# A transformer kernel's gate and up projections as 2x2 block products: seven of 256 columns in place of four of 512

## The chip, the core and the metric

The kernel runs on one core of one Trainium2 chip. Its time is the device time of one execution in microseconds (us). The engines are TensorE (PE in the rows; its weight loads are PEld), VectorE (DVE), ScalarE (ACT), GpSimd (POOL) and SyncE (SP), which issues most of the DMAs. Each engine works through its own list in order; they meet by semaphores.

## What is computed

Two layers of a transformer block and a third block of another kind, on one sequence of 512 tokens and 1024 features. The change is in the feed-forward part of the first two layers:

```python
D_FF = -(-(8 * D_MODEL) // (3 * 256)) * 256        # 2816 = 22 x 128
h2 = rmsnorm(x, norm_ffn[l])
gu = jnp.einsum('btd,df->btf', h2, w_gate_up[l])
g, up = jnp.split(gu, 2, axis=-1)
x = x + jnp.einsum('btf,fd->btd', jax.nn.silu(g) * up, w_down[l])
```

## The kernel before

All of it is kept transposed: features on the 128 partitions, the 512 tokens along a row. Single precision is reached with three matmuls for each block of weights: weights and activations are each split into a rounded part and the rest (`wh`, `wl` and `hh`, `hl`), and `three` and `tile` (L1769 to L1771) add high by high, high by rest and rest by high into one bank of PSUM.

Weights arrive as chunks of 128 x 1024 numbers (512 KB) in a stream that SP loads into two buffers `raw` (L370); ACT rounds a chunk into one of four slots of `wh` (L572), POOL subtracts to get `wl` (L418), and TensorE uses it. The chunks of a layer are those of its mixing part, eight of the output projection (WO), 44 of gate and up and 22 of down. A gate/up chunk holds the 1024 inputs of 128 output features: 8 blocks, so 24 matmuls of 512 columns. A gate chunk and its up chunk are a *pair*; a layer has FT = 22.

The gate/up stage is a loop of 11 trips with two pairs each on TensorE, DVE and ACT. For a pair DVE multiplies both banks with `rstd`, the token's inverse norm (L1384, L1386), ACT takes silu of the gate (L805), DVE multiplies the two (L1389), ACT rounds the product into `ah` (L808), DVE subtracts for `al` (L1391). The four banks go round, so TensorE writes a bank again two pairs later and waits for L1384 or L1386 to have read it. The down stage follows: 22 chunks, each of 24 matmuls with `ah` and `al`, which are kept for all 22 pairs. During it DVE also works at the modulation of the third block: 24 products with the tensor `ada`, loaded by ACT (L1398).

## Time and profile before

| | |
|---|---|
| three timed runs | 2154.14, 2154.64, 2156.37 us (median 2154.64) |
| the profiled execution, first to last instruction | 2152.9 us |
| the same less the median | -1.7 us (its time outside the span is not listed apart) |
| TensorE busy | 2143.8 us (100%), granted clock 1.000 |
| DVE / ACT / POOL busy | 1198.8 (56%) / 939.4 (44%) / 1064.0 us (49%) |
| gate/up stage of layer one and of layer two | from 302.7 to 542.7 and from 958.6 to 1198.9 us |
| DMA | mean 102 GB/s |

A duration of a matmul in the rows is that of one through the whole array; the next one starts before it ends, so the rate is read from the distance of two starts. "Busy" counts such overlap once. The granted clock is 1.00 where TensorE has its full 2.4 GHz.

### The profile page before, as it was taken

What the parts mean: (1) busy time and instruction counts of PE and PEld (TensorE: products, weight loads), DVE (VectorE), ACT (ScalarE), POOL (GpSimd) and SP (SyncE); (2) the same over time, 40 slices, a digit from 0 to 9 for tenths busy, and PEclk for the clock granted to TensorE, in tenths of its full rate; (3) what the DMA queues carried; (4) which work ended last, traced back from release to release, by engine and by line L of the source; (5) the groups of instructions that cost most, each with busy time, mean ns of one, the idle gap of its engine ahead of it and who ended that gap; (6) DMA issues with size and microseconds to landing.
All of it is one profiled execution on the core that took longest, in us unless ns stands there. A gap on an engine that the chain in (4) does not pass through costs nothing.

```text
span 2152.9 us, 29052 instructions
## 1 busy us (share of the span) xinstructions
PE 2143.8 (100%) x10406; PEld 1727.3 (80%) x10406; DVE 1198.8 (56%) x1581; ACT 939.4 (44%) x1517; POOL 1064.0 (49%) x559
## 2 busy tenths in 40 slices
PE   9999999999999999999999999999999999999999
PEld 7877788888888877788888888877787678888887
DVE  7988863222446987864222445759887746333201
ACT  5656543222214556634333215426645655444311
POOL 4973335444444983344444453433766754444442
PEclk9999999999999999999999999999999999999999
DMA  5432223333753332233333672322221012333332
GB/s 184 112 92 68 78 79 112 94 96 97 235 194 97 104 97 69 69 98 98 93 94 95 208 224 85 98 70 68 77 90 50 30 59 89 104 94 94 98 98 88
DMA packets 62869, 219.57 MB, mean 102 GB/s; under 512 B 7936, under 2 KB 8192, under 8 KB 62784
## 3 DMA queue, kind: packets, MB, share of 16 engines
q1 hardware_dynamic: 55728, 193.25, 29.1%
q10 hardware_dynamic: 7056, 25.17, 3.6%
q8 instruction: 54, 0.88, 0.2%
q14 instruction: 31, 0.25, 0.0%
HBM read 212.76 MB, written 2.10 MB: 100 GB/s over the span
## 4 chain that ended last, share of the span: by engine, by line
PE 94%; DVE 3%; POOL 2%; ACT 1%; issue 1%; POOLq 0%; DVEq 0%; ACTq 0%
PE bank L1769 29%; PE bank L1771 28%; PE bank L1770 28%; PE bank L1953 1%; PE bank L1979 1%; PE bank L2014 1%; POOL soft_lo L516 1%; PE bank L1987 0%; DVE soft_hi L1659 0%; POOL wl L418 0%; PE bank L2267 0%; PE bank L2342 0%; PE bank L2398 0%; DVE bank L1620 0%; PE bank L1861 0%
## 5 line engine op out<-in xcount | busy, mean ns | idle before, releaser
L418 POOL TENSOR_TENSOR wl<-raw,wh 128x1024 fp32r<-128x1024 f32 x317 | 771.8, 2436 | 849.3 <-ACT wh L572 849.2
L1769 PE MATMUL bank<-hh,wh 128*128 128x512 f32 (+1 forms) x1979 | 772.1, 390 | 0.9 <-DVE hl L1469 0.6
L1771 PE MATMUL bank<-hh,wl 128*128 128x512 f32 (+1 forms) x1979 | 762.7, 385 | 0.0
L1770 PE MATMUL bank<-hl,wh 128*128 128x512 f32 (+1 forms) x1979 | 762.2, 385 | 0.0
L572 ACT ACTIVATE wh<-raw 128x1024 fp32r<-128x1024 f32 x349 | 368.0, 1055 | 574.3 <-PE bank L1771 509.8
L1769 PEld LDWEIGHTS bank<-hh,wh 128*128 128x128 f32 x1979 | 371.8, 188 | 81.3 <-issue 7.2
L1770 PEld LDWEIGHTS bank<-hl,wh 128*128 128x128 f32 x1979 | 372.0, 188 | 75.1 <-issue 2.2
L1771 PEld LDWEIGHTS bank<-hh,wl 128*128 128x128 f32 x1979 | 371.7, 188 | 75.1
L1769 PE MATMUL bank<-ah,wh 128*128 (+1 forms) x512 | 199.2, 389 | 0.0
L1770 PE MATMUL bank<-al,wh 128*128 (+1 forms) x512 | 199.2, 389 | 0.0
L1771 PE MATMUL bank<-ah,wl 128*128 (+1 forms) x512 | 199.2, 389 | 0.0
L425 POOL TENSOR_TENSOR wl<-raw,wh 128x512 fp32r<-128x512 f32 x64 | 85.2, 1353 | 133.1 <-ACT wh L572 133.1
L1160 DVE SCALAR_TENSOR_TENSOR bank<-glu,par,bank 128x512 f32<-128x512 f32 x180 | 135.9, 755 | 5.8
L1386 DVE TENSOR_TENSOR tmp<-bank,rstd 128x512 f32<-128x512 f32 x44 | 30.4, 691 | 188.2 <-PE bank L1771 188.2
L1769 PEld LDWEIGHTS bank<-ah,wh 128*128 128x128 f32 x512 | 96.1, 188 | 20.1
L1770 PEld LDWEIGHTS bank<-al,wh 128*128 128x128 f32 x512 | 96.1, 188 | 20.0
L1771 PEld LDWEIGHTS bank<-ah,wl 128*128 128x128 f32 x512 | 96.1, 188 | 19.8
L1398 DVE SCALAR_TENSOR_TENSOR ada_acc<-ada_w,cond,ada_acc 128x1024 f32<-128x1024 f32 x42 | 64.8, 1544 | 83.2 <-DMA ada_w<-ada 82.6
L808 ACT ACTIVATE ah<-tmp 128x512 f32 x44 | 27.8, 631 | 182.5 <-DVE tmp L1389 182.5
L710 ACT ACTIVATE prob<-bank,neg_max,q_scale 128x128 f32<-128x128 f32 x128 | 56.9, 454 | 74.2 <-DVE neg_max L1228 74.2
L440 POOL TENSOR_TENSOR conv<-conv,th 128x512 f32<-128x512 f32 x60 | 77.6, 1294 | 13.6 <-ACT th L644 9.3
L1384 DVE TENSOR_TENSOR tmp<-bank,rstd 128x512 f32<-128x512 f32 x44 | 30.4, 690 | 91.5 <-PE bank L1771 90.9
(391 smaller groups left out, 2734.6 us busy)
## 6 DMA issues: line engine op xcount, KB each, us to landing
raw<-stream SPq DMA_DIRECT2D x351, 512.0 KB, 3.6
ada_w<-ada ACTq DMA_DIRECT2D x48, 512.0 KB, 4.6
x<-x_t SPq DMA_DIRECT2D x4, 512.0 KB, 6.9
out_t<-x SPq DMA_DIRECT2D x8, 256.0 KB, 2.1
th<-q SPq DMA_DIRECT2D x16, 64.0 KB
th<-q SPq DMA_DIRECT2D x64, 16.0 KB
q<-th SPq DMA_DIRECT2D x16, 64.0 KB, 2.0
cst<-consts SPq DMA_DIRECT2D x1, 640.0 KB, 5.8
```

Of the source, the lines that this page charges most:

```text
L418: nc.gpsimd.tensor_tensor(wl[:, slot, :], raw[:, raw_slot, :], wh[:, slot, :].bitcast(F32), ALU.subtract).then_inc(lo_ready, 1)
L425: last = nc.gpsimd.tensor_tensor(wl[:, slot, at], raw[:, raw_slot, at], wh[:, slot, at].bitcast(F32), ALU.subtract)
L440: nc.gpsimd.tensor_tensor(conv[:, 1, :], conv[:, 1, :], th[:, 0, 4 + (j - 1) % 4, :], ALU.add).then_inc(tap_added, 1)
L572: af(wh[:, slot, :], raw[:, raw_slot, :], ACT.Copy).then_inc(hi_ready, 1)
L710: af(prob[:, g % 2, i, :], folded[:, i, :], ACT.Exp, bias=neg_max[:, g % 2, i:i + 1], scale=q_scale[:, at:at + 1], accum_out=den[:, g % 2, ...
L1160: link(stt(acc, glu[:, t, j:j + T], w, acc, ALU.mult, ALU.add))
L1384: tt(tmp[:, 2 + p, :], bank[:, b, :], rstd[:, :], ALU.mult).then_inc(lin_free, 1)
L1386: tt(tmp[:, 4 + p, :], bank[:, b + 1, :] if b < 3 else bank[:, 0, :], rstd[:, :], ALU.mult).then_inc(lin_free, 1)
L1398: stt(acc, w, c_k, acc, ALU.mult, ALU.add).then_inc(ada_used, 1)
L1769: mm(dst, wh[:, slot, w], xh, start=start, stop=False)
L1770: mm(dst, wh[:, slot, w], xl, start=False, stop=False)
L1771: return mm(dst, wl[:, slot, w], xh, start=False, stop=stop)
```

## The change

The gate/up stage of the two layers treats a pair as a 2x2 block product. The weights' blocks are: the first and the second half of the 1024 inputs, by gate and up. The activations' blocks are: the first and the second half of the inputs, by the left and the right 256 tokens. Where the plain product takes eight block products (here 48 matmuls of 512 columns, each of which does two of them at once), seven products of sums of blocks are enough. Each product is now 4 blocks x 3 matmuls of 256 columns.

- POOL forms four sums and differences of a pair's weight blocks, `mix` (`mix_up`, `mix_firsts`, `mix_three`, `mix_four`, each 128x512). Together with three blocks taken as they are they are the seven *items* of a pair.
- ACT rounds each item into a half slot of `wh` (`item_round`), DVE subtracts for the rest (`item_rest`; the first ten are done by POOL). Seven half slots go round, so an item is rounded once the same product of the pair before is done. The activations' sums (`set_h`, `set_l`) are made once in each layer, while WO runs.
- TensorE's order for pair p is: first(p), fifth(p), fourth(p-1), third(p-1), sixth(p), second(p), seventh(p). Two sets of three banks alternate between the pairs. Partial results that are used twice are copied out of PSUM by ACT (`snap`) and added by DVE (`gate_first_half`, `up_second_half`, `gate_second_half`), and `activate` multiplies up by silu(gate) in two halves. It reads the first bank of the pair; `first_product` of the pair two later writes this bank and waits for it.
- The products of gate and up are kept whole in `act_full`; scaling by `rstd`, rounding and the rest move into the down stage (`scale_act`, `act_hi`, `act_rest`), with four slots, between the 24 products with `ada`.
- The gate/up weights come from a tensor of their own, `ffn`, into four buffers. The loops of the stage are written out. Several semaphores are merged.

```diff
+        ITEM_HALF = [2, 4, 5, 6, 7, 0, 1]
+        S1, S3, S2, S4 = 0, 1, 2, 3
...
+                        sp.wait_ge(item_lo, n0 + at_second(p - 2))
+                        sp.wait_ge(mixed, s0 + N_SUMS * (p - 1))
+                    sp.dma_start(gate_raw(p), ffn[l * 2 * FT + 2 * p]).then_inc(tile_in[2 * (p % 2)], 16)
...
+                    elif p:
+                        sp.wait_ge(item_lo, n0 + at_fourth(p - 2))
+                    sp.dma_start(up_raw(p), ffn[l * 2 * FT + 2 * p + 1]).then_inc(tile_in[2 * (p % 2) + 1], 16)
...
+                def mix_up(p):
+                    pool.wait_ge(tile_in[2 * (p % 2) + 1], l * PAIR_LOADS + pair_landed(p))
+                    if p:
+                        pool.wait_ge(mixed, s0 + N_SUMS * p)
+                        pool.wait_ge(item_lo, n0 + at_fifth(p - 1))
+                    nc.gpsimd.tensor_tensor(mix[:, S1, :], up_raw(p)[:, 0:T], up_raw(p)[:, T:D], ALU.add).then_inc(mixed, 1)
...
+                def mix_four(p):
+                    pool.wait_ge(mixed, s0 + N_SUMS * p + 3)
+                    if p:
+                        pool.wait_ge(item_lo, n0 + at_third(p - 1))
+                    nc.gpsimd.tensor_tensor(mix[:, S4, :], gate_raw(p)[:, T:D], mix[:, S2, :], ALU.subtract).then_inc(mixed, 1)
...
+                for p in range(2, FT):
+                    mix_up(p)
+                    mix_firsts(p)
+                    mix_three(p)
+                    mix_four(p)
...
+                def item_round(n, src):
+                    if n > 7:
+                        act.wait_ge(product_done, n0 + n - 7)
+                    af(item_of(wh, n), src, ACT.Copy).then_inc(item_hi, 1)
...
+                def snap(p, i, dst):
+                    act.wait_ge(product_done, n0 + [at_first(p), at_sixth(p), at_seventh(p)][i])
+                    af(dst, bank[:, PAIR_BANKS[p % 2][0], LEFT], ACT.Copy).then_inc(snapped, 1)
...
+                for p in range(1, FT):
+                    more = p + 1 < FT
+                    snap(p, 0, sums_tmp(p)[:, LEFT])
+                    if more:
+                        round_first(p + 1)
+                        round_mixed(p + 1, S1, at_fifth(p + 1))
+                        round_fourth(p)
+                        round_mixed(p, S4, at_third(p))
...
+                    snap(p, 1, sums_tmp(p)[:, RIGHT])
+                    if more:
+                        round_mixed(p + 1, S2, at_sixth(p + 1))
+                    silu(p - 1)
+                    if more:
+                        round_second(p + 1)
...
+                    snap(p, 2, up_tmp(p)[:, LEFT])
+                    if more:
+                        round_mixed(p + 1, S3, at_seventh(p + 1))
...
-                with dve.Fori(0, FT // 2) as i:
-                    for p in range(2):
-                        b = (M_GU + 2 * p) % 4
-                        dve.wait_ge(used, i * 4 + (cg + 2 * p + 1))
...
+                def item_rest(n, src):
+                    dve.wait_ge(item_hi, n0 + n)
+                    tt(item_of(wl, n), src, item_of(wh, n).bitcast(F32), ALU.subtract).then_inc(item_lo, 1)
...
+                def up_second_half(p):
+                    dve.wait_ge(product_done, n0 + at_seventh(p))
+                    dve.wait_ge(snapped, 3 * (FT * l + p) + 3)
+                    dve.wait_ge(set_lo, set0 + N_SETS)
+                    tt(up_tmp(p)[:, RIGHT], up_tmp(p)[:, LEFT], bank[:, PAIR_BANKS[p % 2][2], LEFT], ALU.add).then_inc(pair_step, 1)
+
+                def gate_second_half(p):
+                    dve.wait_ge(product_done, n0 + at_third(p))
+                    tt(gate_tmp(p)[:, RIGHT], sums_tmp(p)[:, RIGHT], bank[:, PAIR_BANKS[p % 2][2], LEFT], ALU.add).then_inc(pair_step, 1)
+                    dve.wait_ge(pair_step, gate_second(l, p))
+                    tt(gate_tmp(p), gate_tmp(p), rstd[:, :], ALU.mult).then_inc(pair_step, 1)
+
+                def activate(p):
+                    dve.wait_ge(ffn_silu, FT * l + p + 1)
+                    tt(act_full[:, p, LEFT], bank[:, PAIR_BANKS[p % 2][0], LEFT], gate_tmp(p)[:, LEFT], ALU.mult)
+                    dve.wait_ge(pair_step, up_second(l, p))
+                    tt(act_full[:, p, RIGHT], up_tmp(p)[:, RIGHT], gate_tmp(p)[:, RIGHT], ALU.mult).then_inc(ffn_act, 1)
...
+                    item_rest(at_fourth(p), up_raw(p)[:, T:D])
+                    gate_second_half(p - 1)
+                    item_rest(at_third(p), mix[:, S4, :])
+                    if more:
+                        item_rest(at_sixth(p + 1), mix[:, S2, :])
...
+                    activate(p - 1)
+                    gate_first_half(p)
+                    if more:
+                        item_rest(at_second(p + 1), gate_raw(p + 1)[:, T:D])
+                    up_second_half(p)
+                    if more:
+                        item_rest(at_seventh(p + 1), mix[:, S3, :])
...
-                with pe.Fori(1, FT // 2) as i:
-                    for s in range(4):
-                        pe.wait_ge(lin_free, i * 4 + (mg + s - 3))
-                        tile(i * 4 + (cg + s), (cg + s) % RW, (M_GU + s) % 4, hh, hl)
...
+                def product(n, dst, xh, xl, start, before=lambda kk: None):
+                    pe.wait_ge(item_lo, n0 + n)
+                    high, low = item_of(wh, n), item_of(wl, n)
+                    for kk in range(4):
+                        before(kk)
+                        w = slice(kk * P, kk * P + P)
+                        mm(dst, high[:, w], xh[:, kk, :], start=start and kk == 0, stop=False, skip_group_check=not start)
+                        mm(dst, high[:, w], xl[:, kk, :], start=False, stop=False, skip_group_check=not start)
+                        last = mm(dst, low[:, w], xh[:, kk, :], start=False, stop=kk == 3, skip_group_check=not start)
+                    last.then_inc(product_done, 1)
...
+                def first_product(p):
+                    if p >= 2:
+                        pe.wait_ge(ffn_act, FT * l + p - 1)
+                    product(at_first(p), bank_of(p, 0), hh[:, 0:4, LEFT], hl[:, 0:4, LEFT], True,
...
+                def third_product(p):
+                    pe.wait_ge(pair_step, up_second(l, p))
+                    product(at_third(p), bank_of(p, 2), hh[:, 4:8, RIGHT], hl[:, 4:8, RIGHT], False)
+
+                for p in range(FT):
+                    first_product(p)
+                    fifth_product(p)
+                    if p:
+                        fourth_product(p - 1)
+                        third_product(p - 1)
+                    sixth_product(p)
+                    if p == 0:
+                        sum_of_squares(s0 + SQ_FFN + KT - 1)
+                    second_product(p)
+                    seventh_product(p)
```

The places at which it moves instructions:

DVE before, one pair in the loop of the gate/up stage (L1384 and L1386 read the banks of gate and up; L1391 is the rest of the activations):

```order
L1384 TENSOR_TENSOR tmp<-bank,rstd 128x512 [waits used]
L1385 REGISTER_ALU
L1386 TENSOR_TENSOR tmp<-bank,rstd 128x512 [waits used]
L1387 ISA
L1388 REGISTER_ALU [waits ffn_silu]
L1389 TENSOR_TENSOR tmp<-tmp 128x512 [waits lin_free]
L1391 ISA [waits ah_ready]
L1391 TENSOR_TENSOR al<-tmp,ah 128x512
```

DVE now, one pair in the middle of the stage (L1694 is `item_rest`, L1713 and L1715 `gate_second_half`, L1719 and L1721 `activate`, L1703 `gate_first_half`, L1709 `up_second_half`):

```order
L1694 TENSOR_TENSOR wl<-raw,wh 128x512 [waits item_hi]
L1694 TENSOR_TENSOR wl<-mix,wh 128x512 [waits item_hi]
L1694 TENSOR_TENSOR wl<-pair_raw,wh 128x512 [waits item_hi]
L1713 TENSOR_TENSOR tmp<-tmp,bank 128x256 [waits product_done]
L1715 TENSOR_TENSOR tmp<-tmp,rstd 128x512 [waits pair_step]
L1694 TENSOR_TENSOR wl<-mix,wh 128x512 [waits item_hi] x2
L1719 TENSOR_TENSOR act_full<-bank,tmp 128x256 [waits ffn_silu]
L1721 TENSOR_TENSOR act_full<-tmp 128x256 [waits pair_step]
L1703 TENSOR_TENSOR tmp<-tmp,bank 128x256 [waits ffn_act,snapped,product_done]
L1694 TENSOR_TENSOR wl<-raw,wh 128x512 [waits item_hi]
L1709 TENSOR_TENSOR tmp<-tmp,bank 128x256 [waits set_lo,snapped,product_done]
L1694 TENSOR_TENSOR wl<-mix,wh 128x512 [waits item_hi]
```

Four instructions on 128x512 have become seven rests, one scaling and five instructions on 128x256, and `activate` stands behind the rests of items whose rounding ACT has yet to do.

ACT before, one pair in the loop (L805 silu, L572 the rounding of a chunk, L808 that of the activations):

```order
L805 ACTIVATE tmp<-tmp 128x512 [waits lin_free]
L569 ISA
L571 REGISTER_ALU [waits raw_in0]
L572 ACTIVATE wh<-raw 128x1024 [waits used]
L807 ISA
L808 ISA [waits ffn_act]
L808 ACTIVATE ah<-tmp 128x512
L571 REGISTER_ALU [waits raw_in1]
L572 ACTIVATE wh<-raw 128x1024 [waits used]
```

ACT now, one pair (L981 `snap`, L962 `item_round`, L1026 silu):

```order
L981 ACTIVATE tmp<-bank 128x256 [waits product_done]
L962 ACTIVATE wh<-raw 128x512 [waits product_done,tile_in2]
L962 ACTIVATE wh<-mix 128x512 [waits product_done,mixed]
L962 ACTIVATE wh<-pair_raw 128x512 [waits product_done,tile_in1]
L962 ACTIVATE wh<-mix 128x512 [waits product_done,mixed]
L981 ACTIVATE tmp<-bank 128x256 [waits product_done]
L962 ACTIVATE wh<-mix 128x512 [waits product_done,mixed]
L1026 ACTIVATE tmp<-tmp 128x512 [waits pair_step]
L962 ACTIVATE wh<-raw 128x512 [waits product_done]
L981 ACTIVATE tmp<-bank 128x256 [waits product_done]
L962 ACTIVATE wh<-mix 128x512 [waits product_done,mixed]
```

Silu stands now behind the second `snap`, which waits for the sixth product, and one rounding. What was two waits on TensorE for a pair are ten on `product_done`.

POOL subtracted for two chunks of 128x1024 in each pair before; now it does the four sums of the next pair, in the order `mix_up`, `mix_firsts`, `mix_three`, `mix_four`.

## Rows read from the trace of the kernel before

**Rows 1.** The page: busy time, share of the span, instructions of TensorE.
```profile
PE 2143.8 (100%) x10406; PEld 1727.3 (80%) x10406; DVE 1198.8 (56%) x1581; ACT 939.4 (44%) x1517; POOL 1064.0 (49%) x559
```

**Rows 2.** The page's chain of waits: shares of the span by engine.
```profile
PE 94%; DVE 3%; POOL 2%; ACT 1%; issue 1%; POOLq 0%; DVEq 0%; ACTq 0%
```

**Rows 3.** Windows: gate/up and down stage of layer one, granted clock third from last.
```profile
303.00:542.70 239.70, 239.70 (x1057) 198.13 (x1056) 71.68 (x91) 73.91 (x93) 105.98 (x44) 1.00 0.31 96
542.70:662.40 119.70, 119.70 (x529) 99.10 (x529) 52.14 (x45) 25.27 (x25) 54.94 (x22) 1.00 0.63 202
```

**Rows 4.** Timeline of PE (start, duration, name): matmuls of 512 columns, back to back.
```profile
1198.91 0.39 PE L1769 MATMUL bank<-ah,wh 128*128 128x512 f32 x1
...
1204.35 0.39 PE L1769 MATMUL bank<-ah,wh 128*128 x1
```

**Rows 5.** The same with 256 columns, third block.
```profile
1327.63 0.28 PE L1769 MATMUL bank<-hh,wh 128*128 128x256 f32 x1
...
1330.03 0.28 PE L1771 MATMUL bank<-hh,wl 128*128 128x256 f32 x1
```

**Rows 6.** Groups by shape: busy us, mean ns of one, idle time before.
```profile
L1391 DVE TENSOR_TENSOR al<-tmp,ah 128x512 f32 x44 | 36.9, 838 | 43.1 <-ACT ah L808 43.1
L808 ACT ACTIVATE ah<-tmp 128x512 f32 x44 | 27.8, 631 | 182.5 <-DVE tmp L1389 182.5
L493 POOL TENSOR_TENSOR square_lo<-tmp,square_hi 128x512 fp32r<-128x512 f32 x16 | 20.6, 1291 | 27.4 <-ACT tmp L944 27.4
L736 ACT ACTIVATE q<-bank 128x256 f32<-128x256 f32 x32 | 12.1, 378 | 0.4 <-PE bank L1987 0.4
L1433 DVE TENSOR_TENSOR x<-x,bank 128x256 f32<-128x256 f32 x4 | 1.6, 414 | 0.1
```

**Rows 7.** Timeline of DVE and POOL in the third block's gate/up stage.
```profile
1834.68 0.69 DVE L1752 TENSOR_TENSOR tmp<-tmp 128x512 f32<-128x512 f32 x1
1835.10 2.53 POOL L418 TENSOR_TENSOR wl<-raw,wh 128x1024 fp32r<-128x1024 f32 x1 [1.98 <-ACT wh L572]
...
1836.32 1.85 DVE L1754 TENSOR_TENSOR al<-tmp,ah 128x512 f32 x1 [0.95 <-ACT ah L1053]
```

**Rows 8.** The same, end of the WO stage: both start together.
```profile
298.67 2.96 DVE L1103 SCALAR_TENSOR_TENSOR hl<-x,par,hh 128x512 fp32r<-128x512 f32 x1
298.68 2.39 POOL L418 TENSOR_TENSOR wl<-raw,wh 128x1024 fp32r<-128x1024 f32 x1 [3.05 <-ACT wh L572]
```

**Rows 9.** The same, first pair of layer one: two of POOL in a row.
```profile
321.33 5.20 POOL L418 TENSOR_TENSOR wl<-raw,wh 128x1024 fp32r<-128x1024 f32 x2 [14.82 <-ACT wh L572]
...
322.05 2.23 DVE L1391 TENSOR_TENSOR al<-tmp,ah 128x512 f32 x1 [0.93 <-ACT ah L808]
...
324.20 0.68 DVE L1384 TENSOR_TENSOR tmp<-bank,rstd 128x512 f32<-128x512 f32 x1
```

**Rows 10.** Timeline of DVE and ACT within one pair of layer one.
```profile
348.05 0.69 DVE L1389 TENSOR_TENSOR tmp<-tmp 128x512 f32<-128x512 f32 x1
348.88 0.63 ACT L808 ACTIVATE ah<-tmp 128x512 f32 x1 [4.68 <-DVE tmp L1389]
349.41 1.04 ACT L572 ACTIVATE wh<-raw 128x1024 fp32r<-128x1024 f32 x1
349.66 0.69 DVE L1391 TENSOR_TENSOR al<-tmp,ah 128x512 f32 x1 [0.91 <-ACT ah L808]
```

**Rows 11.** Timeline: last matmul of a chunk and its reader on DVE.
```profile
357.78 0.39 PE L1771 MATMUL bank<-hh,wl 128*128 128x512 f32 x1
...
358.21 0.69 DVE L1386 TENSOR_TENSOR tmp<-bank,rstd 128x512 f32<-128x512 f32 x1 [4.75 <-PE bank L1771]
```

**Rows 12.** Timeline: TensorE resumes behind DVE's two halves of L1433.
```profile
1317.27 0.75 DVE L1433 TENSOR_TENSOR x<-x,bank 128x256 f32<-128x256 f32 x2
...
1317.74 0.39 PE L2099 MATMUL bank<-ah,wh 128*128 128x256 f32 x1 [0.28 <-DVE x L1433]
1317.96 0.28 PE L2100 MATMUL bank<-al,wh 128*128 128x256 f32 x1
```

**Rows 13.** The line of the weight loads, L370.
```profile
DMA to landing us min/median/max: 3.1/3.6/4.9
```

513 lines of the change are left out of this document (401 added, 112 removed).

## The prediction

> **What bounds the kernel now.** I read the page's busy times first: TensorE is busy for 2143.8 of 2152.9 us [rows 1], and the chain of waits gives it 94% of the span [rows 2]. The windows then say where the change lies: TensorE is busy without a gap in the gate/up stage (239.7 of 239.7 us) and in the down stage, at a granted clock of 1.00, its full 2.4 GHz, while DVE is busy for 72 and POOL for 106 us of the same 240 [rows 3]. So the stage costs what its matmuls cost, and the other engines are free of charge as long as they keep up. The question is what fewer matmuls save and whether the others still keep up.
>
> **TensorE's part.** Two starts 24 matmuls apart lie 5.44 us apart: a matmul of 512 columns costs 0.2267 us [rows 4]. With 256 columns, 20 steps take 2.40 us: 0.120 us, a little over half [rows 5]. A pair took 48 x 0.2267 = 10.88 us; seven products of 12 matmuls take 84 x 0.120 = 10.08 us. 0.80 us saved in each of 44 pairs is 35.2 us, if nothing waits. The run of [rows 5] is short and the new one is 22 pairs long, written out; the bound above is the whole duration of one, 0.28 us, that below is 0.120. I take the measured 0.120.
>
> **The other engines' part.** By duration [rows 6], a pair costs DVE seven rests and a scaling at 0.69 us (L1391 has 0.69 undisturbed [rows 10]) and five half operations at 0.41: 7.6 of 10.08 us. ACT has seven roundings and silu at 0.63 and three snaps at 0.38: 6.2 us. POOL has four sums at 1.29: 5.2 us. Each fits alone. DVE and POOL do not run freely beside each other, though. In [rows 7] DVE's L1754 (both inputs in SBUF) starts 1.22 us into a POOL subtraction; POOL ends at 1837.63 and DVE at 1838.17, 0.54 us later. L1752 ends 0.27 us into the same POOL instruction, which takes 2.53 us instead of 2.39 [rows 8]: 2.26 us from DVE's end, so its start-up is 0.13. So one waits for the other, and only a start-up overlaps: a DVE instruction on 512 elements holds the way for 0.54 us, on 256 half of that, 0.27, and POOL's of 1.29 for about 1.16. Started together, POOL goes first [rows 8]; of two POOL instructions in a row DVE gets in between; and L1384, with an input in PSUM, takes 0.68 us under a POOL instruction and so waits for nothing [rows 9].
>
> **Where it meets TensorE.** The tight wait is that of first(p+1) for activate(p-1): it writes the bank that activate reads. Between the end of third(p-1) and the start of first(p+1) TensorE has three products, 4.32 us. I walk that stretch, with 0 at the start of first(p), so third(p-1) ends at 5.76 and first(p+1) should start at 10.08. Signals: a reader on DVE starts 0.20 us after the next matmul could start [rows 11]; ACT to DVE 0.15, DVE to ACT 0.14, and instructions in a row start 0.10 (ACT) before the one ahead ends [rows 10]; I take 0.08 for DVE and 0.1 for other signals.
> - DVE: gate_second_half 5.96 to 6.37, scaling 6.41 to 7.10, rest of third(p) 7.02 to 7.71.
> - That rest releases mix_four(p+1): POOL 7.8 to 9.1.
> - ACT: sixth(p) ends at 7.20; snap 7.40 to 7.78, the rounding of sixth(p+1) 7.68 to 8.31, silu 8.21 to 8.84.
> - DVE: the rest of sixth(p+1) could start at 8.46, waits for POOL, and ends at 9.10 + 0.54 = 9.64. Then activate's left half (an input in PSUM) 9.56 to 9.97; the right half (both in SBUF) issues at 9.90.
> - mix_up(p+2) waits for a weight load that the rest of fourth(p) released at about 6.04; loads take 3.1 to 4.9 us, median 3.6 [rows 13]. It is ready at 6.04 + 3.6 + 0.1 = 9.74, just ahead of the right half, and holds the way until 9.8 + 1.2 = 11.0. The right half ends at 11.3. With a load of 3.1 us POOL goes at 9.64, and the half ends at 11.07.
> - TensorE resumes 0.06 us behind the end of DVE's first half (1317.27 + 0.41), and its first step is 0.22 instead of 0.12 us [rows 12]: 0.16 together. First(p+1) is late by 11.3 + 0.16 - 10.08 = 1.38, or by 1.15; I take 1.3.
> - A load slower than about 3.8 us lets the right half go first: 9.90 + 0.41 + 0.16 = 10.47, late by 0.39.
>
> The lateness returns in each pair, since third(p) follows first(p+1) at a fixed distance. I take seven pairs in ten for the first order: 0.7 x 1.3 + 0.3 x 0.39 = 1.03 us. Pairs 0 and 1 of a layer don't wait, so 20 do: 40 x 1.03 = 41 us, more than the 35 us saved. Queued behind activate on DVE are the rests of second and seventh(p+1), each needed by TensorE some eight us later; that is slack enough.
>
> A rule of the Trainium skill speaks to this, "SBUF — State Buffer", section "SBUF: two separate sides": DVE with two SBUF inputs and a GpSimd instruction that reads SBUF exclude each other, and the loser blocks for the whole instruction. This trace agrees that they exclude each other, but only 0.54 of DVE's 0.69 us is added behind POOL [rows 7]. By the rule to the letter the blocked rest would end at 9.10 + 0.69 = 9.79, mix_up at 11.09, the right half at 11.50, and 1.58 us a pair would be lost in place of 1.03: -35.2 + 63 + 5 = +33, an estimate of 2188 us, near the last rival's, with which its chance stands.
>
> **The stage's edges.** At its start the plain product needed only the rests of the last tile. Now sixth(0) waits for ACT's copy of the first product's bank, which stands behind six ACT operations. From the end of WO: 0.20 + 0.69 (x) + 0.14, then five at 0.53 and one at 0.28 and the snap's 0.38, to 4.3 us; TensorE has 2.88 us of work. That is 1.5 us, and the rests of the last tile, with POOL in the way, lie on the same stretch: 1.5 to 5, I take 2.5 a layer, 5 us in all. At its end, chunk 0 of down takes the banks in an order that leaves the last pair's for last (3.4 us later), which covers gate_second_half, silu and activate (some 3 us): nothing. Before, both edges were without a gap [rows 3].
>
> **The down stage.** It gets 18 x 2 DVE instructions of 0.69 us: 52.1 + 24.8 = 77 us; and if each of POOL's 54.9 us blocked DVE, 132 of 119.7 us [rows 3]. Four slots let the rests run three chunks, 3 x 5.44 = 16 us, behind what TensorE has finished. 132 - 16 is under 119.7, so I put it at nothing; without the slots it would be 12 us in a layer. The merged semaphores and the new weight tensor move no instruction that TensorE waits for.
>
> **Sum.** -35.2 + 41.1 + 5 = +10.9 us. The profiled execution spans 2152.9 us, 1.7 below the median; the difference is added to the median: 2154.6 + 10.9 = 2165.5 us.
>
> **Rivals.**
> - *The right half goes first in every pair*, because loads are later or the rest of sixth(p+1) earlier than in my walk: -35.2 + 40 x 0.39 + 5 = -14.6, 2140 us. For it: only 0.1 to 0.2 us separate the two orders. Against it: the median of 3.6 us lies on the other side.
> - *TensorE never waits in the stage.* Without POOL the rest of sixth(p+1) ends at 9.15 and the right half at 9.8. That needs mix_four out of the way by 8.5 and mix_up after 9.9. -35.2 + 5 = -30, 2124.5 us. Against it is [rows 7].
> - *256-column matmuls don't hold 0.120 us* over a long written-out stretch. At 0.1295 a pair is at 10.88 again. The saving is gone, but so is the wait's hold: about 2155 us. Nothing in [rows 5] speaks for it.
> - *DVE and POOL are the bound.* DVE's 7.6 us and POOL's 4 x 1.16 in one row, less four start-ups of 0.15 us, is 11.6; with signals 11.8. It decides once DVE has no idle time left in a pair; my walk leaves it about a microsecond. 40 x 1.72 - 35.2 + 5 = +38.6, 2193 us.
>
> **Numbers.** A change within 0.2%, 4.3 us, can't be told from none. Forecast 0.42 (own range 2159 to 2180), right half first 0.20, no wait 0.16, the 256-column rate 0.09, DVE and POOL the bound 0.13. Slower: 0.42 + 0.13 = 0.55. Faster: 0.20 + 0.16 = 0.36. Same: 0.09. The range reaches into the third and the last rival, each about half, 2126 to 2190.
>
> **What would show it.** Right: matmuls of 256 columns at 0.120 us; pairs of 11.0 to 11.4 us; TensorE idle before first_product, released by DVE's second half of activate; that half at 1.0 us or more on average where 0.41 would do; DVE busy about 80% of the stage and POOL about 45%. The first rival shows as pairs of 10.5 us with that half at 0.41, the second as a stage without gaps, the last as DVE without idle time and TensorE waiting for item rests. The forecast is wrong if TensorE's waits in the stage sum to under 30 us, or if more than 10 us are lost in the down stage.

## The result, and the profile after

The changed kernel takes 2201.47 us (median of 4 runs, 2201.14 to 2202.71) against 2154.47 for the kernel before: 1.0217 of its time, 95% interval 1.0203 to 1.0232. It is slower, as forecast, but by 47 us where the forecast was 11, and outside the range given. Times are medians; stage times and rows are those of one profiled execution, which can lie some us off its median (the text says where it matters).

The page of the profile after, its busy times and its chain of waits, which answer to [rows 1, 2]:

```profile
PE 2135.6 (97%) x11990; PEld 1783.6 (81%) x11990; DVE 1615.6 (73%) x2101; ACT 1079.5 (49%) x1899; POOL 1165.9 (53%) x667
PE 64%; DVE 15%; issue 11%; POOL 6%; ACT 3%; DMA 0%; POOLq 0%; ACTq 0%; SPq 0%; DVEq 0%
```

TensorE is busy for 8 us less, the span is 47 us more, 2199.9 us, and DVE's share of the chain has gone from 3 to 15%. The windows of the gate/up and the down stage of layer one, columns as in [rows 3]:

```profile
302.90:550.20 247.30, 230.71 (x1852) 225.01 (x1851) 221.34 (x298) 135.93 (x257) 147.00 (x92) 0.98 0.29 90
550.20:681.80 131.60, 123.60 (x530) 99.49 (x528) 105.07 (x79) 33.43 (x42) 56.27 (x23) 0.99 0.54 187
```

Both stages ran without a gap before, in 239.7 and 119.7 us. Now TensorE idles for 17 and for 8 us in them, and DVE is busy for 90 and 80% of them. In us: gate/up from its first matmul to the first of down, down from there to its last matmul, and mixing 2 from that one to the first of WO; WO of layer two, 43.69 us in both kernels, is left out:

| | gate/up 1 | down 1 | mixing 2 | gate/up 2 | down 2, start of third block |
|---|---|---|---|---|---|
| before | 240.27 | 119.45 | 252.53 | 240.27 | 121.82 |
| after | 247.32 | 131.59 | 255.68 | 246.34 | 139.06 |
| difference | +7.1 | +12.1 | +3.2 | +6.1 | +17.2 |

These are 45.7 of the 47.0 us. So the 35.2 us that TensorE saves are more than spent in gate/up itself, and most of the loss lies in the down stage, for which the forecast had nothing. The +3.2 of mixing is for the most part a wait of 2.2 us at its start. In the last column lies one wait of 6.6 us, and the granted clock was 0.50 from 1349.3 to 1356.2 us around its end. What TensorE waited for, from the view of waits (us in total, times, longest):

```profile
PE bank L2442 <- ACT tmp L981: 17.7, 6, 7.8
PE bank L2442 <- DVE act_full L1721: 14.1, 40, 2.3
PE bank L2152 <- POOL wl L530: 7.5, 8, 1.5
PE bank L2548 <- POOL wl L530: 6.6, 1, 6.6
PE bank L2152 <- DVE act_full L1721: 3.6, 2, 2.3
PE bank L2152 <- DVE al L1730: 2.9, 3, 2.0
PE bank L2152 <- DVE hl L1375: 2.2, 1, 2.2
```

The first two rows are the gate/up stage (mostly the first snap of a layer, 7.8 us twice, and activate's second half), the others the down stage and its edges.

**A pair in the steady stretch.** Timeline of PE, then of DVE and POOL, around one first product:

```profile
429.35 0.39 PE L2442 MATMUL bank<-hh,wh 128*128 128x256 f32 x1 [0.28 <-DVE act_full L1721]
...
439.97 0.39 PE L2442 MATMUL bank<-hh,wh 128*128 128x256 f32 x1 [0.28 <-DVE act_full L1721]
```

```profile
434.70 1.43 DVE L1694 TENSOR_TENSOR wl<-raw,wh 128x512 fp32r<-128x512 f32 x1 [0.27 <-ACT wh L962]
436.05 0.41 DVE L1713 TENSOR_TENSOR tmp<-tmp,bank 128x256 f32<-128x256 f32 x1
...
437.11 1.37 DVE L1694 TENSOR_TENSOR wl<-mix,wh 128x512 fp32r<-128x512 f32 x2
438.39 0.42 DVE L1719 TENSOR_TENSOR act_full<-bank,tmp 128x256 f32<-128x256 f32 x1
438.73 1.19 DVE L1721 TENSOR_TENSOR act_full<-tmp 128x256 f32<-128x256 f32 x1
...
433.84 1.74 POOL L608 TENSOR_TENSOR mix<-mix,pair_raw 128x512 f32<-128x512 f32 x1
437.94 1.70 POOL L614 TENSOR_TENSOR mix<-pair_raw,mix 128x512 f32<-128x512 f32 x1 [2.36 <-DVE wl L1694]
439.77 1.30 POOL L596 TENSOR_TENSOR mix<-raw 128x512 f32<-128x512 f32 x1
```

A pair takes 10.62 us: 10.08 of matmuls (they hold 0.120 us apart) and 0.54 of lateness. Activate's right half (L1721), with both inputs in SBUF, takes 1.19 us instead of 0.42, while POOL's mix_four (L614) is running; mix_up (L596) comes only afterwards. Further up, mix_three (L608) makes the rest of fourth take 1.43 us instead of 0.69, so gate_second_half (L1713) starts 6.70 us after first_product. 0.28 us of the wait is idle time, the rest a slow first step.

**The start of the stage.** DVE's last addition to x and its work up to the last split, ACT's snap, and TensorE, in three pieces:

```profile
307.51 0.68 DVE L1684 TENSOR_TENSOR x<-x,bank 128x512 f32<-128x512 f32 x1
309.05 1.37 DVE L1659 TENSOR_TENSOR tmp<-act_full 128x256 f32<-128x256 f32 x1 [0.85 <-ACT act_full L1001]
310.34 1.48 DVE L1660 TENSOR_TENSOR tmp<-act_full,g_left 128x256 f32<-128x256 f32 x1
```

```profile
312.72 0.61 ACT L962 ACTIVATE wh<-mix 128x512 fp32r<-128x512 f32 x1
313.24 0.36 ACT L981 ACTIVATE tmp<-bank 128x256 f32<-128x256 f32 x1
```

```profile
313.66 0.58 PE L2442 MATMUL bank<-set_h,wh 128*128 128x256 f32 x1 [7.78 <-ACT tmp L981]
314.04 0.41 PE L2443 MATMUL bank<-set_l,wh 128*128 128x256 f32 x1
314.25 0.41 PE L2444 MATMUL bank<-set_h,wl 128*128 128x256 f32 x1
```

WO's last matmul is followed by the first product at 302.85, so the last addition could start at 303.05. It starts at 307.51, behind DVE's earlier work. Two subtractions (L1659, L1660) that took 0.43 and 0.42 us for the tile ahead take 1.37 and 1.48 under POOL's instructions, and the snap comes at 313.24. TensorE waits 7.78 us, and when it resumes its matmuls lie 0.21 us apart instead of 0.12. The windows of the same place show why (granted clock third from last):

```profile
302.90:308.20 5.30, 2.98 (x25) 2.78 (x23) 4.45 (x10) 3.73 (x7) 2.47 (x2) 1.00 0.33 99
308.20:318.50 10.30, 4.84 (x16) 3.81 (x17) 6.34 (x7) 6.56 (x12) 8.28 (x7) 0.50 0.00 0
```

The granted clock is at half, 1.2 GHz, from 308.3 us on, 2.4 us into TensorE's idle time, and up to 318.5; for half of this stretch TensorE was waiting anyway, for 4.8 us it worked. Layer two waits as long (7.80 us) and works 5.8 us at half clock (991.96 to 997.8).

**The down stage.** Timeline of ACT with its queue, then of DVE and POOL, from one chunk to the next:

```profile
600.65 0.63 ACT L1033 ACTIVATE ah<-act_full 128x512 fp32r<-128x512 f32 x1 [7.57 <-DVE ada_acc L1776]
601.19 1.05 ACT L739 ACTIVATE wh<-raw 128x1024 fp32r<-128x1024 f32 x1
606.05 0.33 ACTq L1084 DMA_DIRECT2D ada_w<-ada  x1
606.48 0.63 ACT L1033 ACTIVATE ah<-act_full 128x512 fp32r<-128x512 f32 x1 [4.25 <-DVE ada_acc L1774]
```

```profile
601.38 0.69 DVE L1730 TENSOR_TENSOR al<-act_full,ah 128x512 fp32r<-128x512 f32 x1 [1.20 <-ACT ah L1033]
601.99 0.69 DVE L1725 TENSOR_TENSOR act_full<-act_full,rstd 128x512 f32<-128x512 f32 x1
602.59 3.42 DVE L1774 SCALAR_TENSOR_TENSOR ada_acc<-ada_w,cond,ada_acc 128x1024 f32<-128x1024 f32 x1
607.22 0.69 DVE L1730 TENSOR_TENSOR al<-act_full,ah 128x512 fp32r<-128x512 f32 x1 [1.20 <-ACT ah L1033]
...
602.31 2.63 POOL L530 TENSOR_TENSOR wl<-raw,wh 128x1024 fp32r<-128x1024 f32 x1 [6.53 <-ACT wh L739]
```

Follow it round: DVE's modulation product (L1774) ends at 606.01; ACT's DMA issue for the next modulation load, which waits for that buffer, goes at 606.05; the rounding of act (L1033), which stands behind it in ACT's list, at 606.48; DVE's rest of it (L1730), ahead of the next product in DVE's list, at 607.22. The ring takes 5.84 us (601.38 to 607.22) where TensorE needs 5.44 for a chunk. DVE is idle for 1.20 us of it.

A part of the ring is POOL's. The product lasts 3.42 us here, and 1.28 us in the 13 places where no POOL instruction runs beside it: it starts 0.28 us into POOL's subtraction for the chunk (L530), which ACT's rounding ahead of it (L739) released, and is held for 2.14 us. 29 of the 42 such products took over 1.5 us, against 6 of 42 before, where the page has

```profile
L1398 DVE SCALAR_TENSOR_TENSOR ada_acc<-ada_w,cond,ada_acc 128x1024 f32<-128x1024 f32 x42 | 64.8, 1544 | 83.2 <-DMA ada_w<-ada 82.6
```

(mean 1.54 us; now 2.61). Without this hold the turn would be some 3.7 us, an estimate from these rows (5.84 less 2.14), and shorter than a chunk. No run took POOL's part away by itself.

### The profile page after: what moved, and what is told of

The parts are those of the page before. It is cut to its first block, busy times and chain, and to the rows that moved or that the text cites. A ratio compares the mean times of both kernels' runs of the same rounds, so it can differ in the third digit from the quotient of the medians.

```text
span 2199.9 us, 32833 instructions
## 1 busy us (share of the span) xinstructions
PE 2135.6 (97%) x11990; PEld 1783.6 (81%) x11990; DVE 1615.6 (73%) x2101; ACT 1079.5 (49%) x1899; POOL 1165.9 (53%) x667
## 4 chain that ended last, share of the span: by engine, by line
PE 64%; DVE 15%; issue 11%; POOL 6%; ACT 3%; DMA 0%; POOLq 0%; ACTq 0%; SPq 0%; DVEq 0%
PE bank L2152 16%; PE bank L2154 16%; PE bank L2153 16%; DVE wl L1694 5%; POOL wl L530 5%; PE bank L2442 3%; PE bank L2444 3%; PE bank L2443 3%; DVE act_full L1721 2%; DVE tmp L1715 1%; ACT wh L962 1%; PE bank L2336 1%; PE bank L2362 1%; PE bank L2397 1%; DVE act_full L1719 1%
## 5 line engine op out<-in xcount | busy, mean ns | idle before, releaser
L530 POOL TENSOR_TENSOR wl<-raw,wh 128x1024 fp32r<-128x1024 f32 x229 | 562.7, 2459 | 606.8 <-ACT wh L739 606.6
L2152 PE MATMUL bank<-hh,wh 128*128 128x512 f32 (+1 forms) x1275 | 498.3, 391 | 3.6 <-DVE hl L1375 2.2
L2154 PE MATMUL bank<-hh,wl 128*128 128x512 f32 (+1 forms) x1275 | 489.6, 384 | 0.0
L2153 PE MATMUL bank<-hl,wh 128*128 128x512 f32 (+1 forms) x1275 | 488.9, 383 | 0.0
L739 ACT ACTIVATE wh<-raw 128x1024 fp32r<-128x1024 f32 x261 | 275.0, 1055 | 376.7 <-PE bank L2154 307.6
L2442 PE MATMUL bank<-hh,wh 128*128 128x256 f32 x704 | 205.2, 291 | 14.1 <-DVE act_full L1721 14.1
L2152 PE MATMUL bank<-ah,wh 128*128 128x512 f32 (+1 forms) x512 | 201.7, 394 | 13.6 <-POOL wl L530 6.9
L2153 PE MATMUL bank<-al,wh 128*128 128x512 f32 (+1 forms) x512 | 200.0, 391 | 0.0
L2154 PE MATMUL bank<-ah,wl 128*128 128x512 f32 (+1 forms) x512 | 199.8, 390 | 0.0
L2444 PE MATMUL bank<-hh,wl 128*128 128x256 f32 x704 | 199.6, 284 | 0.0
L2443 PE MATMUL bank<-hl,wh 128*128 128x256 f32 x704 | 199.5, 283 | 0.0
L1694 DVE TENSOR_TENSOR wl<-mix,wh 128x512 fp32r<-128x512 f32 x164 | 135.2, 827 | 20.1 <-ACT wh L962 20.1
L962 ACT ACTIVATE wh<-mix 128x512 fp32r<-128x512 f32 x176 | 110.3, 627 | 57.5 <-PE bank L2444 55.3
```

The lines of the kernel that those rows point to most:

```text
L530: nc.gpsimd.tensor_tensor(wl[:, slot, :], raw[:, raw_slot, :], wh[:, slot, :].bitcast(F32), ALU.subtract).then_inc(lo_ready, 1)
L739: af(wh[:, slot, :], raw[:, raw_slot, :], ACT.Copy).then_inc(hi_ready, 1)
L962: af(item_of(wh, n), src, ACT.Copy).then_inc(item_hi, 1)
L1694: tt(item_of(wl, n), src, item_of(wh, n).bitcast(F32), ALU.subtract).then_inc(item_lo, 1)
L2152: mm(dst, wh[:, slot, w], xh, start=start, stop=False)
L2153: mm(dst, wh[:, slot, w], xl, start=False, stop=False)
```

## The experiments

The experiments ask what costs the down stage its time, what makes activate late, what sets the start of the stage, and whether the parts add. Each is the changed kernel with the edit shown. A time is the median of four runs, of ten for e10, twelve for e9 and e11 and five for e13; ratios are to the kernel before.

**1. Modulation loads issued by SyncE (e1).** ACT's issues, with their wait, go to SyncE's list, between the down stage's refills.

```diff
-                    act.wait_ge(ada_used, 24 * l + a - 1)
-                act.dma_start(ada_w[:, a % 2, :], ada[24 * l + a]).then_inc(ada_in[a % 2], 16)
+                    sp.wait_ge(ada_used, 24 * l + a - 1)
+                sp.dma_start(ada_w[:, a % 2, :], ada[24 * l + a]).then_inc(ada_in[a % 2], 16)
```

> The 24 loads of ada of a layer are issued by SP, between its weight loads, in place of ACT; nothing else changes. Theory A (a ring of waits: in ACT's list each ada load waits for DVE's product two before, and the rounding that DVE's next rest needs stands behind that load): the ring is cut, the down stages of the two layers, now 12.1 and 17.2 us longer than before the change, lose at least two thirds of that; 2201.5 falls to 2178 to 2185 us, and ACT's rounding L1033 no longer sits idle for ada_acc. Theory B (DVE and POOL hold up each other in the down stage, whoever issues loads): DVE's and POOL's instructions are the same, so it stays within 4 us of 2201.5.

Measured: 2177.97 us, ratio to before 1.0121 (1.0089 to 1.0153), 23.5 us less than the changed kernel; its runs spread widely, from 2172.6 to 2187.81. The down stage takes 123.57 us and with the start of the third block 123.14, mixing 252.24. Every wait of TensorE for L530 is gone; DVE has all its work still:

```profile
550.00:673.60 123.60, 121.41 (x530) 100.04 (x529) 101.25 (x82) 37.25 (x45) 59.96 (x24) 0.99 0.59 204
```

So the stage was bound by the ring through ACT's list, not by the sum of DVE's and POOL's work: DVE is busy for 101 us (105 without the edit), its holds by POOL included, and that fits. Fewer holds are left, too: a product takes 1.85 us on average, not 2.61.

**2. The modulation products on 8 columns (e2).** The opposite end of the ring; most of the modulation is left out. The edit reaches 42 of the 48 products (the first of each sum of eight is another instruction), each on 8 of its 1024 columns, not of 1,536.

```diff
-                        stt(acc, w, c_k, acc, ALU.mult, ALU.add).then_inc(ada_used, 1)
+                        stt(acc[:, 0:8], w[:, 0:8], c_k, acc[:, 0:8], ALU.mult, ALU.add).then_inc(ada_used, 1)
```

> The changed kernel with the 48 modulation products of DVE (L1774) on 8 of 1,536 columns: that part of the computation is left out, the order of all instructions and all waits are kept. It measures how much of the down stage's loss hangs on the length of that product. Theory A (a ring of waits: ACT's load waits for the product two before, DVE's rest waits for the rounding that stands behind this load): with a product of 0.1 instead of 3.2 us the ring turns faster than a chunk and the stage is back at 120 to 124 us in both layers, a gain of 2 x 10 to 2 x 13 us: about 2178 us, as when SyncE issued the loads. Theory B (the load's own flight of 3 to 5 us sets the ring): the period falls by only part of the 3 us, down stays over 126 us, and the time is over 2190 us. A second effect counts for both: mixing of the next layer begins without DVE's backlog.

Measured: 2182.65 us, 1.0131 (1.0101 to 1.0162). Down takes 124.04 and 123.44 us. Either end of the ring opened gives the same stage, to 0.5 us; theory A holds for the stage. Its premise of a product of 0.1 us does not: 0.23 us free, but mostly longer under POOL, 1.16 on average:

```profile
604.69 2.36 DVE L1774 SCALAR_TENSOR_TENSOR ada_acc<-ada_w,cond,ada_acc 128x8 f32<-128x8 f32 x1
```

So the edit took about 1.1 us off a held product, and that was enough. The median is 5 us over e1's, within the spread of both (here 2173.08 to 2193.98); between the two profiles layer one's gate/up stage makes the difference, 254.35 us in this one (see 3).

**3. The last pair's silu first (e3).** At the end of gate/up TensorE waited 2.27 us for the last activate, whose silu stood on ACT behind a rounding that waits for a weight load.

```diff
-                round_chunk(c0 + C_DN + 2)
                 silu(FT - 1)
+                round_chunk(c0 + C_DN + 2)
```

> The last pair's silu stands ahead of the rounding of the third down chunk in ACT's list, not behind it. Theory A (silu waits for a weight load that it does not need; TensorE then waits 2.27 us for the last activate and runs at half clock for 3.4 us after it): both go in both layers, 2 x (2.3 + 1.7) = 8 us, 2193.5 us. Theory B (the last activate is late because of POOL's two long subtractions on the same way): under 3 us, and the wait for L1721 stays.

Measured: 2204.73 us (2199.61 to 2210.3), 1.0225. The wait is gone, and the first down stage takes 129.39 us instead of 131.59; but the 8 us of theory A did not show in the time. The profile is that of the slowest run, and its layer one needed 254.51 us for gate/up, 7.2 more, though nothing was edited there. One early wait for activate was 3.03 us long instead of 2.27, the clock fell, and of the next eight pairs the first took 12.7 us and the others 11.3 to 11.5:

```profile
334.00:336.80 2.80, 2.80 (x15) 2.80 (x15) 2.24 (x3) 0.24 (x1) 1.17 (x2) 0.50 0.19 22
```

```profile
380.48 0.39 PE L2442 MATMUL bank<-hh,wh 128*128 128x256 f32 x1 [1.01 <-DVE act_full L1721]
391.77 0.39 PE L2442 MATMUL bank<-hh,wh 128*128 128x256 f32 x1 [0.95 <-DVE act_full L1721]
```

```profile
377.57 1.38 DVE L1694 TENSOR_TENSOR wl<-mix,wh 128x512 fp32r<-128x512 f32 x1 [0.62 <-ACT wh L962]
...
379.20 1.23 DVE L1721 TENSOR_TENSOR act_full<-tmp 128x256 f32<-128x256 f32 x1
...
377.09 1.31 POOL L614 TENSOR_TENSOR mix<-pair_raw,mix 128x512 f32<-128x512 f32 x1 [3.00 <-DVE wl L1694]
378.87 1.27 POOL L596 TENSOR_TENSOR mix<-raw 128x512 f32<-128x512 f32 x1 [0.47 <-DMA raw<-ffn]
```

The first fence is a window behind that wait, with the clock granted at 0.50; the second has first(p+1) of two pairs in a row; the third DVE and POOL ahead of one of them. Here mix_four blocks the rest of sixth, and mix_up, released by its load, gets in 0.33 us ahead of the right half. This is the order of the forecast's walk. The loop was seen in two orders that repeat themselves; the forecast's is the one that it leaves after some pairs, and 10.62 us the one in which it stays. In e2's profile the same wait is again 3.03 us, and that stage 254.35.

**4. The right half of up in PSUM (e4).** For pairs 0 to 19 the second half of up goes into bank 3, so that both halves of activate have an input in PSUM.

```diff
+        def up_right(p):
+            return bank[:, 3, (p % 2) * HALF:(p % 2) * HALF + HALF] if p < FT - 2 else up_tmp(p)[:, RIGHT]
-                    tt(up_tmp(p)[:, RIGHT], up_tmp(p)[:, LEFT], bank[:, PAIR_BANKS[p % 2][2], LEFT], ALU.add).then_inc(pair_step, 1)
+                    tt(up_right(p), up_tmp(p)[:, LEFT], bank[:, PAIR_BANKS[p % 2][2], LEFT], ALU.add).then_inc(pair_step, 1)
-                    tt(act_full[:, p, RIGHT], up_tmp(p)[:, RIGHT], gate_tmp(p)[:, RIGHT], ALU.mult).then_inc(ffn_act, 1)
+                    tt(act_full[:, p, RIGHT], up_right(p), gate_tmp(p)[:, RIGHT], ALU.mult).then_inc(ffn_act, 1)
```

> up_second_half writes into a free bank of PSUM for pairs 0 to 19, so that activate's right half has one input in SBUF in place of two. Theory A (in the middle of the stage the right half waits for POOL's fourth sum, 1.19 us in place of 0.41, and nothing else makes first_product wait): a pair falls from 10.62 to 10.08 or little above (10.2), 40 x 0.4 to 0.54: 2180 to 2185 us. Theory B (what the right half no longer waits for, the next rests wait for, and the chain behind gate_second_half stays late): a pair at 10.4 to 10.6, 2194 to 2201 us.

Measured: 2182.5 us (2181.7 to 2187.46), 1.0128 (19 less than the changed kernel). Layer two's gate/up takes 235.77 us, with pairs 10.08 us apart; layer one's 243.09 in this profile, which is that of the slowest run: behind a fall of the clock at 335 us one pair took 12.0 us and the next eight 10.6 to 10.8. Why they stayed longer isn't shown. The half itself, under a running mix_four:

```profile
1107.20 0.41 DVE L1724 TENSOR_TENSOR act_full<-bank,tmp 128x256 f32<-128x256 f32 x1
...
1106.37 1.73 POOL L617 TENSOR_TENSOR mix<-pair_raw,mix 128x512 f32<-128x512 f32 x1 [2.95 <-DVE wl L1697]
```

0.41 us instead of 1.19, and at most 0.42 in all 40 pairs so changed: with an input in PSUM it isn't blocked, and the steady wait is gone.

**5. POOL's sums on 8 of 512 columns (e6).** From pair 1 on; the mixed weights are left mostly uncomputed.

```diff
-                    nc.gpsimd.tensor_tensor(mix[:, S4, :], gate_raw(p)[:, T:D], mix[:, S2, :], ALU.subtract).then_inc(mixed, 1)
+                    nc.gpsimd.tensor_tensor(mix[:, S4, 0:T if p == 0 else 8], gate_raw(p)[:, T:D if p == 0 else T + 8], mix[:, S2, 0:T if p == 0 else 8], ALU.subtract).then_inc(mixed, 1)
...
```

> POOL forms its four sums on 8 of 512 columns for pairs 1 to 21 (pair 0 whole), so the products of these pairs are left partly undone; all waits stay. Theory A (what holds first_product back in the middle of the stage is POOL's sums on the way that it shares with DVE): a pair falls from 10.62 to 10.08 us in both layers, 40 x 0.54 = 21.6 us less, and DVE's mean for a rest falls to 0.69; with the sums of pair 1 gone from the stage's start up to 3 us a layer more: 2174 to 2180 us. Theory B (the chain of ACT and DVE, sixth product, snap, rounding, silu, activate, is too long by itself): a pair stays at 10.4 us or more, over 2192 us.

Measured: 2176.53 us, 1.0094 (25 less). From pair 3 on every pair is 10.08 us long, a rest on DVE takes 0.69 us on average as theory A has it, and gate/up takes 232.08 and 233.54 us. TensorE still waits for the first snap, for 5.8 instead of 7.8 us, so POOL's sums of pair 1 are 2 us of that. It agrees with e4: DVE alone keeps up with 10.08 us; POOL's hold on the way to SBUF is all of the steady wait.

**6. The start: DVE's order (e5).** DVE adds x(t) ahead of the splits of the tile before.

```diff
+                    dve.wait_ge(used, c0 + C_WO + t + 1)
+                    tt(x[:, t, :], x[:, t, :], bank[:, t % 4, :], ALU.add).then_inc(x_new, 1)
...
-                    dve.wait_ge(used, c0 + C_WO + t + 1)
-                    tt(x[:, t, :], x[:, t, :], bank[:, t % 4, :], ALU.add).then_inc(x_new, 1)
```

> In the output projection DVE adds tile t to x before it does the sums and rests of tile t-1, not after. Theory A (DVE's list puts the addition, on which ACT's scaling and then three more DVE instructions wait, behind work that nobody waits for yet; the last addition is 4.7 us late and TensorE waits 7.8 us in each layer): the last addition comes within 1 us of the tile's end and the wait of sixth(0) falls to 3 to 4 us, the clock does not fall: 2 x (4 + 2.4), 2201.5 to about 2188. Theory B (DVE is simply full, since POOL's sums and rests lie on the same way): the order changes little, 0 to 4 us.

Measured: 2203.89 us, 1.0227. The last addition comes at 305.55 instead of 307.51, and TensorE waits 8.3 us, not less. That is theory B. The splits now behind the additions are needed as well, so the amount of work seems to matter and not its order; that is argued here, and 7 bears on it.

**7. POOL's ten item rests on 8 columns, in layer two only (e7).** Part of the low halves of these weights is left out.

```diff
+                    w = 8 if l else T
-                    nc.gpsimd.tensor_tensor(item_of(wl, n), src, item_of(wh, n).bitcast(F32), ALU.subtract).then_inc(item_lo, 1)
+                    nc.gpsimd.tensor_tensor(item_of(wl, n)[:, 0:w], src[:, 0:w], item_of(wh, n)[:, 0:w].bitcast(F32), ALU.subtract).then_inc(item_lo, 1)
```

> In layer two alone POOL does its ten item rests on 8 of 512 columns (layer two's first items keep old low parts); layer one is as it was. Theory A (DVE is late with the last tiles of the output projection because POOL's rests and sums hold the shared way): layer two's wait for the first snap falls from 7.8 to 2 to 4 us and its half clock shortens, while layer one keeps 7.8; 5 to 8 us in all, 2193 to 2197 us. Theory B (DVE's own list of sums and rests is too long for a tile's 5.44 us): layer two's wait stays at 6 us or more.

Measured: 2197.52 us, 1.0196 (4 less than the changed kernel). Layer one is the control: it waits 7.8 us again. Layer two waits 3.0:

```profile
987.45 0.58 PE L2443 MATMUL bank<-set_h,wh 128*128 128x256 f32 x1 [3.00 <-ACT tmp L982]
```

Its gate/up takes 240.83 us against 246.34 in the changed kernel. So 4.8 of the 7.8 us hang on POOL's rests. With e6, where POOL's sums of pair 1 were worth 2.0 us of the same wait, POOL's share may be larger; the two edits were not made together.

**8. Pair 0's sums earlier (e8).** They go between POOL's last rests of WO, to empty its queue at the start.

```diff
-                rests(c0 + C_GATE + 16 + RW, c0 + C_DN)
+                rests(c0 + C_GATE + 16 + RW, c0 + C_DN - 4)
+                last_rest(c0 + C_DN - 4)
+                last_rest(c0 + C_DN - 3)
                 mix_firsts(0)
+                last_rest(c0 + C_DN - 2)
...
```

> POOL forms pair 0's sums between its last rests of the output projection's chunks, up to 7 us earlier, instead of behind them. Theory A (it is the crowding of POOL and DVE in tiles 4 to 7 that costs): some 5 us of POOL's work leaves the crowded stretch, the wait of sixth(0) falls from 7.8 to 3 to 5 us in each layer: 2190 to 2196 us. Theory B (DVE's own list is too long): within 2 us of 2201.5.

Measured: 2208.45 us, 1.0272. The wait is 10.2 us in layer one and 9.8 in layer two: both theories missed. That the sums now block DVE where it is already behind with the splits is the likely cause, but not shown.

**9. All four together (e10).** e1, e3, e4 and e8.

> Four edits together: ada loads issued by SP, the last silu ahead of the chunk's rounding, the second half of up in PSUM, pair 0's sums early. If the losses are at separate places they add up: 2201.5 - 23.5 - 19 - 4 to 8 (the last silu) - 6 to 10 (the start of the stage) = 2141 to 2149 us, below the kernel before the change (2154.4). If they are one shortage of DVE and POOL that moves on to the next place when one is mended, less than 45 us goes: 2156 us or more.

Measured: 2153.44 us, 0.9998 (0.9986 to 1.0009). The down stages are back at 119.48 and 121.85 us, as before the change (123.57 and 123.14 with e1's edit alone), and gate/up takes 238.4 and 238.6. The start's wait is 9.9 us in layer one and 10.9 in layer two. The time lies between the two theories' (2149 and 2156), and e8's part does harm here as it did alone.

**10. Three together, without e8 (e9).**

> Three edits of earlier runs together: SyncE issues the modulation loads, the last pair's silu stands ahead of the rounding of the third down chunk, and the second half of up lies in a PSUM bank for pairs 0 to 19. The sums of pair 0 stay where the changed kernel has them. Theory A: the parts are independent, and what is left over is the start of each gate/up stage. Then the wait for the first snap is 7.8 us as in the changed kernel, against 10.9 us in the version that also moved the sums of pair 0: two layers give back 2 x 3.1 us from 2153.4, 2147 us. Theory B: the start costs a fixed 10.2 us at half clock whatever the wait is, and the version with the sums moved had made up for its wait elsewhere: 2153, as before the change.

Measured: 2147.65 us (2145.83 to 2160.4), 0.9979 (0.9966 to 0.9991). The wait is 7.8 us and gate/up 236.32 and 235.44: theory A, within 1 us (from e10 the waits fell by 2.1 and 3.1 us, not 3.1 twice). What TensorE still waits for in the two stages:

```profile
PE bank L2452 <- ACT tmp L1000: 17.7, 6, 7.8
PE bank L2452 <- DVE act_full L1731: 2.7, 2, 1.8
```

**11. POOL held back (e11).** e9, and POOL waits for the eleventh split.

```diff
-                mix_up(1)
+                pool.wait_ge(set_lo, N_SETS * l + 11)
                 item_rest(at_seventh(0), mix[:, S3, :])
+                mix_up(1)
```

> The same three edits, and at the end of WO GpSimd is held back: it waits for the eleventh of twelve splits of the activations before the rest of the seventh product of pair 0, the sum of up's blocks of pair 1 comes after that, and ACT's rounding of that sum comes after the first snap. Theory A: DVE's queue at the end of WO is long because GpSimd blocks it; each GpSimd instruction of 1.29 us that is moved behind the last DVE split gives DVE up to 1.2 us. The wait for the first snap falls from 7.8 to about 4 to 5 us in each layer, and the time to about 2141 us. Theory B: DVE has too much work of its own there; the wait stays at 7 us or more, what GpSimd does later is then missing for pair 1, and the time is that of the three edits or up to 5 us more.

Measured: 2148.11 us, 0.9976 (0.9964 to 0.9989), no different from e9. The first wait falls to 4.3 us, as theory A has it, but the time does not. The rows are of a run of 2152.6 us, 4.5 above the median:

```profile
PE bank L2452 <- ACT tmp L1001: 11.0, 7, 4.3
PE bank L2452 <- DVE bank L1719: 5.4, 2, 2.7
```

```profile
325.00:330.80 5.80, 5.80 (x28) 5.80 (x29) 5.77 (x6) 2.30 (x5) 3.78 (x3) 0.50 0.27 90
```

What POOL does later is missing for pair 1: a new wait of 2.7 us, and behind it in layer one a second stretch at half clock, with TensorE busy throughout (5.80 of 5.80 us). In layer two no fall follows the same wait (2.71 us, at 977.0); one of 3.4 us comes behind the next, of 2.26 us, at 985.3.

**12. One rounding behind the first snap (e13).** e9, with ACT's order changed by one operation.

```diff
                     if t == KT - 1:
-                        round_mixed(1, S1, at_fifth(1))
...
                 snap(0, 1, sums_tmp(0)[:, RIGHT])
+                round_mixed(1, S1, at_fifth(1))
```

> The three edits, and only ACT's order at the start of the stage changed: the rounding of pair 1's sum of up stands behind the first snap instead of ahead of it. Theory A: ACT's list decides when the first snap comes; one operation of 0.53 us fewer ahead of it takes 0.5 us off each layer's wait: 1 us less than the three edits alone. Theory B: ACT is idle there and waits for DVE's last addition and splits; the wait is unchanged within 0.1 us, and so is the time.

Measured: 2146.12 us (2144.54 to 2147.39), 0.9956 (0.9943 to 0.9969). The wait is 7.29 us, 0.5 less in each layer, as theory A has it; the 1.5 us between the medians of e13 and e9 are within e9's spread. This version beats both kernels, the one before by 8.4 us:

```profile
538.70:658.20 119.50, 119.50 (x529) 99.00 (x528) 100.08 (x82) 37.51 (x45) 61.47 (x24) 1.00 0.62 211
```

The down stage is full again, with DVE busy for 100 of its 119.5 us where [rows 3] have 52. Of the 35.2 us saved by TensorE, 9.8 arrive (240.27 twice, less 235.91 and 234.87).

## Why the prediction was wrong

Of the 36 us between forecast and result, 29 lie where the forecast had nothing, in the down stages with the third block's start, and 3 in the mixing behind the first. That is the step that failed most: "move no instruction that TensorE waits for". In the gate/up stage two terms were mis-sized in opposite directions.

*TensorE's part, -35.2 us: right.* 256-column matmuls hold 0.120 us at full clock over the stage; e6 has pairs of exactly 10.08 us from pair 3 on. The third rival falls.

*The steady wait, +41.1 us: the mechanism right, the size not.* TensorE waits 40 times for activate's right half, which POOL blocks, and e4 and e6 each take the wait away. But the lateness is 0.54 us a pair, 21.6 in all, not 1.03. The step that failed is the order in the walk. I had mix_four (7.8 to 9.1) over before activate, and mix_up blocking the half. In the steady order mix_three still runs when the rest of fourth should, so gate_second_half starts at 6.70 and not at 5.96, and the rest of third ends at 8.45 and not at 7.71. So mix_four starts later (8.59), the rest of sixth goes ahead of it, and it is mix_four that holds the half for 0.77 us. The order as written exists, for eight pairs of e3's profile, at 11.3 us and more. I had let DVE be free when third(p-1) ends, when the state at the end of a pair should have been carried into the next until it repeated.

*The stage's edges, +5 us: mis-sized, it is some 26.* Gate/up as a whole lost 13.1 us over the two layers; -35.2 + 21.6 leaves 26.7 for starts and ends. Of these 15.6 are the two waits for the first snap, 2.1 four smaller ones, some 3 the first wait for activate in each layer (2.27 and 1.01 us for 0.28), and 5.3 is what TensorE lost while it worked at half clock (half of 4.8 us in layer one and of 5.8 in layer two). The rest, under 1 us, isn't accounted for. I counted ACT's operations from the end of WO and took DVE as free then. It was 4.5 us behind, since the change adds sums and 12 splits to the end of WO, and I had not set these against POOL's time there; e7 gives POOL's rests 4.8 of the 7.8 us. And I had not priced what a wait of TensorE does to its clock, though idle time was what the forecast was about. Because two errors offset each other, the forecast for the gate/up stage (+10.9) is close to what was measured (+13.1); it is not right for that.

*The down stage, 0: wrong, it is +29, and +3 in mixing.* The sum of DVE and POOL was no bad bound: with every hold counted as busy, DVE's time fits, as e1 shows. What failed is "move no instruction that TensorE waits for". The split of act, moved into the down stage, closes a ring: DVE's product, ACT's load that waits for its buffer, the rounding queued behind that wait, DVE's rest ahead of the next product. A turn takes 5.84 us for the 5.44 of a chunk, and 2.14 of them are POOL's hold on the product. I had asked what is queued behind an added wait, but not what the moved operations themselves are queued behind on ACT. Opened at either end (e1, e2) it gives back 8 us in layer one, 16 in layer two with the third block's start, and the 3 of mixing. The end of the stage before it, put at nothing, cost 2.27 us of wait in layer one and a second fall of the clock (1.3 us of wait in layer two); of the 4.1 and 1.3 us that e1 leaves in the two down stages, part is this edge, since e10 and e9, with the last silu first, leave none.

*The forecast's own signs.* TensorE's waits in the gate/up stages sum to 31.8 us, over the 30 named, but about half of them are the first snap's; activate's right half took 1.17 us on average, where 1.0 or more was named, but pairs took 10.62 us and not 11.0 to 11.4. The sign of being wrong that came true is the last, more than 10 us lost in the down stage.

*The lock between DVE and POOL.* The exclusion is confirmed, by e4 above all (one input in PSUM: 0.41 us under POOL). Mix_four ends at 439.64 and the blocked half, which takes 0.42 us by itself, at 439.92, 0.28 later, as I had taken it. The Trainium skill, "SBUF — State Buffer", section "SBUF: two separate sides", has the one that starts first keep the shared ports for its whole instruction while the other fully blocks. The trace agrees with that: mix_four starts first, at 437.94 for 438.73, and the half ends behind it. What it doesn't bear out is my reading "to the letter", by which the blocked one's full length is added behind: 0.28 of 0.42 us was.

*The rivals.* Neither "right half first" nor "never waits" occurred. "DVE and POOL the bound" came nearest in us (2193) and is wrong in cause: e6 has pairs at 10.08 us with all of DVE's own work, and the excess lies in another stage.

Open: why the loop leaves the 11.3 us order after eight pairs; what decides whether a wait of 1.9 to 2.8 us brings the clock down; whether the ring would have cost anything without POOL's hold on the product; and the last 7.3 us of wait at the start, of which only parts of POOL's share were measured.
